# Two transformer blocks on one core: the modulation's products with w_mod move from TensorE to GpSimd and VectorE

## What is computed

```
mod = (silu(c) @ w_mod + b_mod).reshape(6, 1024)           # for x
mc  = (silu(c_ctx) @ w_mod + b_mod).reshape(6, 1024)       # for the context; only mc[0] and mc[1] are used
hc = rmsnorm(ctx, g_mix) * (1 + mc[1]) + mc[0]
f_f, f_b, i_c = split(hc @ w_in[:, :1536])                 # gates and values of the context
s_ctx_f, s_ctx_b = final states of the gated linear attention over the context
h = rmsnorm(x, g_mix) * (1 + mod[1]) + mod[0]
mix = token_mixers(h @ w_in, ..., s_ctx_f, s_ctx_b)        # linear attention both ways, spatial gating, w_pa, w_pb, w_o
x = x + mod[2] * mix
h2 = rmsnorm(x, g_ffn) * (1 + mod[4]) + mod[3]
x = x + mod[5] * swiglu(h2, w_up, w_down)
x = rmsnorm(x, g_final)                                    # then the second block: FFNs and two attentions
```

## Time and profile before

| | |
|---|---|
| three runs, median | 1637.83 us |
| the profiled execution | 1636.97 us |
| its span, first to last instruction | 1635.7 us |
| mean granted TensorE clock | 0.962 |
| busy: TensorE, VectorE, ScalarE, GpSimd | 1540.1, 917.1, 792.2, 47.8 us |
| read from memory | 264.74 MB, 162 GB/s over the span |

### The profile page before, as it was taken

One profiled execution on the slowest core, in us unless ns is written; L12 is line 12 of the kernel. 1 busy time (PEld: TensorE's weight loads), 2 busy tenths in 40 slices (PEclk: granted clock), 3 DMA queues, 4 the chain that ended last, 5 costly groups with the idle time before them and its releaser, 6 DMA issues.

```text
span 1635.7 us, 20070 instructions
## 1 busy us (share of the span) xinstructions
PE 1540.1 (94%) x8188; PEld 1277.9 (78%) x8188; DVE 917.1 (56%) x1294; ACT 792.2 (48%) x1153; POOL 47.8 (3%) x83
## 2 busy tenths in 40 slices
PE   7998999998999999999999999999999777899998
PEld 3897888886888878887898788878888675578886
DVE  2627664877555565555455655556554457365553
ACT  2525435554445355544565555455554444365542
POOL 1000200000000000000021000000000011000000
PEclk9999788999999999999999999999999888799999
DMA  9225353644565655555533455555555410145652
GB/s 380 79 81 204 128 194 129 232 145 163 182 187 186 201 164 186 185 191 180 168 128 126 155 184 184 193 180 179 185 188 190 146 54 26 37 155 183 188 185 103
DMA packets 72236, 267.11 MB, mean 163 GB/s; under 512 B 8016, under 2 KB 8272, under 8 KB 70736
## 3 DMA queue, kind: packets, MB, share of 16 engines
q1 hardware_dynamic: 69984, 258.87, 48.0%
q10 hardware_dynamic: 2160, 6.95, 1.2%
HBM read 264.74 MB, written 1.05 MB: 162 GB/s over the span
## 4 chain that ended last, share of the span: by engine, by line
PE 83%; DVE 8%; ACT 5%; issue 2%; DMA 1%; POOL 0%; ACTq 0%; SPq 0%; DVEq 0%
PE PS L691 20%; PE PS L707 12%; PE PS L709 12%; PE PS L708 12%; PE PS L342 4%; PE PS L343 4%; PE PS L344 4%; DVE WL L1485 2%; ACT WH L991 2%; PE PS L675 1%; PE PS L442 1%; PE PS L374 1%; PE PS L375 1%; PE PS L376 1%; PE PS L563 1%
## 5 line engine op out<-in xcount | busy, mean ns | idle before, releaser
L1485 DVE TENSOR_TENSOR WL<-RAW,WH 128x1024 fp32r<-128x1024 f32 (+1 forms) x472 | 569.9, 1224 | 361.7 <-ACT WH L991 361.2
L991 ACT ACTIVATE WH<-RAW 128x1024 fp32r<-128x1024 f32 (+1 forms) x472 | 484.4, 1053 | 290.6 <-DMA RAW<-in_up 169.9
L707 PE MATMUL PS<-WH,XH 128*128 128x512 f32 x912 | 376.7, 413 | 24.5 <-DVE WL L1485 14.4
L709 PE MATMUL PS<-WH,XL 128*128 128x512 f32 x912 | 357.9, 392 | 0.0
L708 PE MATMUL PS<-WL,XH 128*128 128x512 f32 x912 | 357.7, 392 | 0.0
L707 PEld LDWEIGHTS PS<-WH,XH 128*128 128x128 f32 x912 | 172.2, 189 | 77.3 <-DVE WL L1485 18.3
L709 PEld LDWEIGHTS PS<-WH,XL 128*128 128x128 f32 x912 | 172.0, 189 | 37.0
L708 PEld LDWEIGHTS PS<-WL,XH 128*128 128x128 f32 x912 | 172.6, 189 | 27.7
L691 PE MATMUL PS<-WH,GH 128*128 128x512 f32 x440 | 137.3, 393 | 0.0
L691 PE MATMUL PS<-WL,GH 128*128 128x512 f32 x440 | 135.6, 389 | 0.0
L691 PE MATMUL PS<-WH,GL 128*128 128x512 f32 x440 | 135.6, 389 | 0.0
(11 more groups left out here) (365 smaller groups left out, 2133.8 us busy)
## 6 DMA issues: line engine op xcount, KB each, us to landing
RAW<-in_up SPq DMA_DIRECT2D x220, 512.0 KB, 4.7
RAW<-in_down SPq DMA_DIRECT2D x110, 512.0 KB, 3.2
RAW<-in_win SPq DMA_DIRECT2D x44, 512.0 KB, 5.4
RAW<-in_mod SPq DMA_DIRECT2D x32, 512.0 KB, 4.9
MC<-in_mod SPq DMA_DIRECT2D x8, 1024.0 KB, 16.8
RAW<-in_sbqk SPq DMA_DIRECT2D x16, 512.0 KB, 4.8
GROW<-in_grow ACTq DMA_DIRECT2D x9, 512.0 KB, 4.6
RAW<-in_wo SPq DMA_DIRECT2D x8, 512.0 KB, 3.7
```

What stands on the lines that cost most here:

```text
L707: e.matmul(o_[:, :], l, w[:, s], start=(k == 0), stop=False, skip_group_check=True)
L709: m = e.matmul(o_[:, :], ll, w[:, s], start=False, stop=(k == KD - 1), skip_group_check=True)
L991: e.activation(WH[s][:, 0:c], RAW[s][:, 0:c], ACT.Copy).then_inc(*sig("hi", j))
L1485: e.tensor_tensor(WL[s][:, 0:c], RAW[s][:, 0:c], WH[s][:, 0:c].bitcast(F32), ALU.subtract).then_inc(*sig("lo", j))
```

## The change

The products with w_mod are taken from TensorE, but for five of the first eight chunks.

- **GpSimd** (`mod_part`, in the program of GpSimd) multiplies each 256-column piece of a chunk with the column of silu(c) that belongs to its 128 rows, in place, and adds the eight pieces up to one of 128x256 (ring PM, two tiles). It does so for the context in chunks 5, 7 and 1, into a scratch tile PX, then sums the context's squares as before, and then for x in chunks 8 to 23, from the raw slots, the two masks of the attention in between.
- **VectorE** does the same for x in chunks 5, 7, 1 (ring DM). Chunks 4, 6, 0, 2, 3 stay on TensorE as before, for both vectors.
- **TensorE** then sums over the 128 partitions with a column or matrix of ones (`mod_summed`): one matmul of 256 columns for GROW, two of one column for MOD.
- The chunks of w_mod are not split any more; `split_to` runs four chunks ahead that are not w_mod's. A slot of w_mod is free when GpSimd is done with it.
- The plan places the chunks earlier (`MODS_BEHIND`), and their sums on TensorE and VectorE stand at other tiles (`MODS_END`); 22 and 23 come behind w_pa and w_o.
- x is loaded first; the context behind the first four weight chunks. On TensorE all gate tiles of x (0 and 1, 2, 3) come before those of the context, and the context's `spread` stands behind the former. ScalarE squares the context after it has modulated x.

```diff
+MODS_BEHIND = {3: (8,), 4: (9,), 5: (10, 11), 6: (12,), 7: (13,), 8: (14,), 9: (15,), 10: (16,), 11: (17,), 13: (18,),
+               15: (19,), 17: (20,), 19: (21,)}
+MODS_END = {3: (8,), 5: (9,), 6: (10,), 7: (11,), 8: (12,), 9: (13,), 10: (14,), 11: (15,), 12: (16,), 13: (17,), 15: (18,),
+            17: (19,), 19: (20,), 21: (21,)}
 def weight_plan():
+    plan = []
+    for i in range(22):
         plan += [("win", 2 * i + z, 1024) for z in range(2)]
+        plan += [("mod", 2 * m + z, 1024) for m in MODS_BEHIND.get(i, ()) for z in range(2)]
+    for kind, m in (("wpa", 22), ("wpb", 23)):
+        plan += [(kind, i, 1024) for i in range(4)] + [("mod", 2 * m + z, 1024) for z in range(2)]
...
             # TensorE
+            def mod_summed(name, part, ready):
+                b, empty = bank(("modt", *name), ("mod", *name))
+                pe.wait_ge(*ready)
+                pe.wait_ge(*empty)
+                if name[0] // 4 in (2, 5):
+                    m = e.matmul(b[:, 0:T], ONE, part[:, :], start=True, stop=True)
+                else:
+                    for t in range(2):
+                        m = e.matmul(b[:, t:t + 1], part[:, t * P:(t + 1) * P], ONE[:, 0:1], start=True, stop=True)
             def mods(*chunks):
+                    mod_summed((i,), PM.of(("pa", i)), at("pa", i, 1, 6))
+                    for z in range(2):
+                        used[chunk["mod", 2 * i + z]] = ("pa", i, z, 5 + z)
...
             mod_first(4)
+            sums("nx")
             mod_first(6)
+            mod_turned(4)
+            mod_vector(5)
+            mod_first(0)
+            mod_turned(6)
             spread("nx")
+            mod_vector(7)
+            mod_turned(0)
+            mod_first(2)
+            mod_context(5)
+            mod_vector(1)
+            mod_turned(2)
+            mod_first(3)
+            mod_context(7)
+            mod_turned(3)
+            group = [("win", c, ("fg", 0, c), ("fs", 0, c)) for c in range(2)]
+            for k in range(KD):
+                by_k_step(k, group, HH, HL, at("hl", k))
+            mod_context(1)
+            gates(0, 2)
             sums("nc")
+            gates(0, 3)
+            mods_end(3)
             spread("nc")
+            for c in range(4):
+                gates(1, c)
...
             # GpSimd
+            def mod_part(i, context):
+                part, before = PM.take(("pa", i), ("modt", i, "ctx") if context else ("modt", i))
+                po.wait_ge(*after(before))
+                for z in range(2):
...
+                    for y in range(4):
+                        s, k = slice(y * T, (y + 1) * T), 2 * (4 * z + y) + context
+                        e.tensor_scalar(by[:, s], w[:, s], SILC[:, k:k + 1], None, ALU.mult).then_inc(*sig("pa", i, z, y))
+                    po.wait_ge(*at("pa", i, z, 3))
+                    e.tensor_tensor(by[:, 0:2 * T], by[:, 0:2 * T], by[:, 2 * T:4 * T], ALU.add).then_inc(*sig("pa", i, z, 4))
+                    po.wait_ge(*at("pa", i, z, 4))
+                    if z == 0:
+                        e.tensor_tensor(part[:, :], by[:, 0:T], by[:, T:2 * T], ALU.add).then_inc(*sig("pa", i, z, 5))
+                    else:
+                        e.tensor_tensor(by[:, 0:T], by[:, 0:T], by[:, T:2 * T], ALU.add).then_inc(*sig("pa", i, z, 5))
+                        po.wait_ge(*at("pa", i, z, 5))
+                        e.tensor_tensor(part[:, :], part[:, :], by[:, 0:T], ALU.add).then_inc(*sig("pa", i, z, 6))
+            for last, i in ((None, 5), (5, 7), (7, 1)):
+                mod_part(i, 1)
+            gather("nc")
+            for i in range(8, 16):
+                mod_part(i, 0)
+            gla_mask(0)
+            mod_part(16, 0)
+            mod_part(17, 0)
+            gla_mask(1)
+            for i in range(18, 24):
+                mod_part(i, 0)
...
             # SP
-            for z, i in enumerate(FIRST):
-                if z == 1:
-                    e.dma_start(XF[:, :, :], a["xf"]).then_inc(s_xf, 16)
-                if z == 4:
-                    e.dma_start(XC[:, :, :], a["ctx"]).then_inc(s_ctx, 16)
+            e.dma_start(XF[:, :, :], a["xf"]).then_inc(s_xf, 16)
+            for i in FIRST:
                 e.dma_start(MC[i][:, :], a["mod"][i]).then_inc(s_mod[i], 16)
             for j, (kind, i, cols) in enumerate(plan):
+                if j == 4:
+                    e.dma_start(XC[:, :, :], a["ctx"]).then_inc(s_ctx, 16)
                 if j >= SLOTS:
                     sp.wait_ge(*at(*used[j - SLOTS]))
+                elif j >= 2 and FIRST[j - 2] in ON_PE:
+                    sp.wait_ge(*at("modp", FIRST[j - 2]))
                 elif j >= 2:
-                    sp.wait_ge(*at("modp", FIRST[j - 2]))
+                    sp.wait_ge(*at("da", FIRST[j - 2], KD - 1))
+                    sp.wait_ge(*at("pa", FIRST[j - 2], 1, 6))
```

More of the change, by code:

```diff
@@ L59, in weight_plan, with ahead_of @@
     return plan
+def ahead_of(plan, j):
+    more = [i for i in range(j + 1, min(j + 9, len(plan))) if plan[i][0] != "mod"]
+    return more[:4][-1]
 class Values:
@@ L458, in mods, with mods_end @@
[L458 to L461 removed]
+                    mod_summed((i,), PM.of(("pa", i)), at("pa", i, 1, 6))
+                    for z in range(2):
+                        used[chunk["mod", 2 * i + z]] = ("pa", i, z, 5 + z)
+            def mods_end(tile):
+                mods(*MODS_END.get(tile, ()))
             pe.wait_ge(*CONST)
[L465 removed]
+            pe.wait_ge(*at("act", "silc"))
```

321 lines of the change are left out of this document (150 added, 171 removed).

## The result

The changed kernel takes 1673.78 us (median of 4 runs, 1671.1 to 1674.72) against 1638.3 for the kernel before: a ratio of 1.0209 with an interval of 1.0189 to 1.0229. It is 35 us slower; the forecast was 16 us faster, with a range up to 1655. The whole interval of the ratio lies above 1, so that it is slower is clear of noise.

The account below looks back on a forecast made before the run. TensorE, busy 94% of the span, was taken to bound the kernel; +15 us in the start, -14 in the attention and -17 in the rest gave -16, from 1637 to 1621 us; range 1597 to 1652, with 3 us for the clock.

Parts of the forecast that it names:

- TensorE's saving: Chunks 8 to 23: TensorE loses net 36 us of work, 19 before 249 us and 17 behind.
- The start: Up to the end of the gates: GpSimd's context parts and part 8 make TensorE wait, +15 us.
- The attention, from the gates to its end: Linear attention: 14 of 19 us gained, 5 given back through w_mod slots that GpSimd frees late.
- The price of a part: GpSimd's work on one chunk, eight multiplications and five additions, taken as 8.3 us.
- the selection being the one-input row: GpSimd's multiplication by a column priced like its selection: 0.42 us for 256 columns, 0.37 start to start.
- my upper bound: GpSimd's multiplication of 128x256 by a column costs at most the 724 ns of an addition.
- My slower rival: GpSimd sets the pace in start and attention; at 11.1 us a part, eleven parts on the path, 1652 us; chance 0.23.
- The exclusion: Where both have work, GpSimd's parts and VectorE's two-input work exclude each other, so their times add up.
- the slots behind tiles 9 to 12: Attention: loads of tiles 9 to 12 wait for parts 12 to 15 to free slots; tile 10 at 178, not 171.
- The rest: Projections behind the attention: GpSimd's parts fit in, so the whole 17 us are gained.
- if late they hold up loads: Parts 22 and 23, behind w_pa and w_o: if late, they delay loads of w_o and the first up-projection.
- The clock: Low clock after idle time puts the start's end at 113, not 111; 3 us in the range for added waits.

Follow-up runs that it names:

- e5_few: Changed kernel with only one GpSimd addition of 128x256 per slot left in chunks 8 to 23, rest of the sum left out: 1625.76 us.
- e8_old_few: Changed kernel with the old start and order of the kernel before, and one GpSimd addition per slot in chunks 8 to 23: 1618.11 us.
- e10_few_late: e8_old_few with chunk i of w_mod loaded behind tile i from tile 8 on, sums and masks moved too: 1612.72 us.
- e2_half: Changed kernel with two of each slot's four GpSimd multiplications left out in chunks 8 to 23: 1653.79 us.
- e6_writes: Changed kernel with each GpSimd operation of a part in chunks 8 to 23 replaced by a memset that reads nothing: 1644.84 us.
- e1_wide: Changed kernel with one GpSimd product by a broadcast factor in place of four multiplications by a column: 1670.87 us.
- e4_old_start: Changed kernel with the start and order of the kernel before; chunks 8 to 23 as in the changed kernel: 1656.09 us.

## Why the prediction was wrong

**TensorE's saving (right behind the attention, not shown in it).** Behind the attention the changed kernel takes 60.7 us in place of 78.5: 18 gained, as the 17 forecast. In the attention the forecast was 19, and no run shows them: from the gates to the attention's end e5_few gains 6 us, e8_old_few 3 and e10_few_late 12 (139.7 against 151.6), all with hardly any GpSimd work.

**The start (+15 forecast, +17 measured), right by two errors.** The shape came as told: a first wait of 7.92 us at `mod_context(7)`, a second of 6.45 for part 8, 8.22 for the context's modulation, and the third context part done at 58.8 where 61 was forecast; TensorE reached its sum at 60.16 and had no wait there. But a context part took 15.5 us with its waits where I had 8.3, and VectorE and GpSimd did not add up to the full sum of their work that I had put in: with the measured price, 12.2 + 3 x 12.4 + 24 would be 73.

**The attention, from the gates to its end (-14 forecast, +29 measured), wrong.** Three terms.
- The price of a part: 8.3 in the sum, 12.4 undisturbed. The failed step is "the selection being the one-input row": 128x256 multiplied by a column takes 0.915 us, above my upper bound, which I had taken from an addition in the belief that one input can't be dearer than two. e2_half gives this term 20 us. My slower rival had the mechanism, the place and the formula: with 12.4 in place of 8.3, eleven parts on the path give 1621 + 11 x 4.1 = 1666. It had the price too low, and even this near hit is in part luck: by the formula the start would lose another 16 us and the attention 29, where they lost 1 and 43 more than forecast.
- The exclusion: I let two-input work wait, at the price of VectorE's own work. In fact VectorE's one-input operations take part as well (3.19 us in place of 1.12), even against a GpSimd that only writes (2.94), and the waits fall on the chains that TensorE stands behind. e6_writes against e2_half gives 9 us at equal pace; in e1_wide a quarter less GpSimd work (137 to 102 us) buys 3 us at most, since VectorE's busy time rises from 78 to 101 us.
- The order of the loads: the prediction followed the slots behind tiles 9 to 12 and never asked when tile 7 is split. The statement above that the splits run four chunks ahead leaves out that only eight entries of the plan are looked at, which is what stops them at tile 6. e10_few_late against e8_old_few shows the keys late by 11.5 us through the order (with the sums and masks that move with it), and about 5 us of it at the end. I had read that the splits run only four chunks ahead, and costed it only where GpSimd frees a slot.

**The rest (-17 forecast, -18 measured), right**; behind w_pa another 6 us are lost, which the sum had at nothing. e5_few does not lose them, so they go with the late parts, "if late they hold up loads"; e8_old_few and e10_few_late lose 3 of them without such parts, which stays unexplained.

**The clock (3 us at the range's edge).** The sum let it cost 2 us in the start and nothing in the attention. The granted clock of 0.75 there took back some 12 us by the estimate above.

**The sum by the runs.** From the changed kernel's 1673.8: 17.7 for the start (e4_old_start), 38.0 for GpSimd's pace and exclusion with the old start (e8_old_few against e4_old_start), 5.4 for the order (e10_few_late) lead to 1612.7. Taken in another order the terms differ: GpSimd's work first is worth 48.0 (e5_few), the start then 7.7. What is missing to the 1602 of TensorE's saving alone stays partly open. In e10_few_late the stretch from 138 to 238 us and in before that from 137 to 249 read:

```profile
138.00:238.00 100.00, 93.34 (x609) 84.75 (x608) 54.92 (x78) 33.85 (x45) 17.04 (x17) 0.77 0.38 133
```

```profile
137.00:249.00 112.00, 109.22 (x760) 93.72 (x761) 75.71 (x107) 51.60 (x64) 11.78 (x4) 0.84 0.44 147
```

TensorE is idle 6.7 us in place of 2.8, and its granted clock is 0.77 in place of 0.84. Both point to the same thing, that with the 18 us of w_mod's products gone the chains of the attention are less well covered; but no run separates the two, and this is argued, not shown.

## What to carry to other kernels

Before work goes to an idle engine, price its operation from a row of the same form, with the same kind of scalar and width; where there is none, the next operation that looks dearer is no upper bound: here the multiplication cost 2.5 times the assumed price and a quarter more than the bound, and the range must leave room for that. Ask next what the new work shares with its neighbours: here a three to four times cheaper home was VectorE itself, which looked busier but did a chunk in 3.8 us where GpSimd took 12.4 alone and 15.6 in company. And when chunks are put earlier in a queue of loads with a fixed number of slots, follow the first tile behind them to its load and to its place in the queue of each engine that prepares it, not only the slots that the new work holds.

## What the runs showed of the hardware

- GpSimd, 128x256 of fp32 in SBUF: multiplied by a column 0.915 us, by a constant 0.841, two tensors added 0.72 to 0.74; 128x512 added 1.29. VectorE multiplies by a column in 0.345 us. The Trainium skill (GPSIMD Engine Reference, Engine selection) puts one input near line rate and two at half: here the one-input form is the dearer one.
- A GpSimd memset of 128x1024 takes 0.95 us (mean 0.970 of 128). Beside VectorE's two-input operations both run at their own speed (35 splits of 1.22 us); beside one-input operations from SBUF to SBUF both are held up (memsets up to 1.92 us, VectorE's four from 1.12 to 2.94).
- VectorE's multiply-and-add of 128x256 by a column takes 0.494 us in a dependent series with GpSimd nearly idle.
- The exclusion with a GpSimd that reads goes both ways and takes in VectorE's one-input operations from SBUF to SBUF: 1.12 us became 3.19 for four, 1.23 became 2.06 for 128x2048, while GpSimd's multiplication went from 0.915 to 3.01 at most.
